# Summing the index scores over heads on TensorE with diagonal weight matrices, in a two-block transformer kernel

## The reference, cut to what matters

```python
dots = jnp.einsum('bthd,bsd->bths', qib.astype(f32), k_idx_f)
score = jnp.einsum('bths,bth->bts', jax.nn.relu(dots), wib.astype(f32)) * idx_scale
causal = key_pos[None, :] <= t[:, None]
score = jnp.where(causal[None], score, -jnp.inf)
_, sel = lax.top_k(score, top_k)
```

## Time and profile before

| what | value |
|---|---|
| median of 3 runs | 1260.83 us (1260.47 to 1261.44) |
| the profiled execution's own time | 1259.97 us |
| its span on the core | 1258.3 us |
| busy over the whole span | PE 82%, PEld 48%, DVE 35%, ACT 19%, POOL 3% |
| the stage of the change | about 495 us to 545 us from the span's start |

### The profile page before, as it was taken

How to read it: one execution, slowest core, us unless ns; L and a number is a source line. 1 busy time by engine, 2 the same in 40 slices (tenths; PEclk the granted TensorE clock), 3 DMA queues, 4 the chain that set the end, 5 groups by cost and what they waited for, 6 DMA issues and landing times.

```text
span 1258.3 us, 15368 instructions
## 1 busy us (share of the span) xinstructions
PE 1035.6 (82%) x6153; PEld 604.1 (48%) x6153; DVE 445.6 (35%) x1040; ACT 234.7 (19%) x576; POOL 41.7 (3%) x93
## 2 busy tenths in 40 slices
PE   5999999999999999978999999887474737464647
PEld 1788855444334448766888685632221303121213
DVE  0469827222221156976852462410010101010101
ACT  1233303111111232224512100310101101010101
POOL 0000000000000010100102300000000000000000
PEclk8899899999999999989999989897787878786878
DMA  9885957999999999323113236899999999999997
GB/s 364 283 329 204 395 182 308 394 429 427 427 431 428 416 344 393 125 77 125 68 43 139 102 105 268 344 383 423 425 421 426 419 429 421 429 420 429 419 428 290
DMA packets 80046, 406.13 MB, mean 323 GB/s; under 512 B 18713, under 2 KB 26198, under 8 KB 57336
## 3 DMA queue, kind: packets, MB, share of 16 engines
q1 hardware_dynamic: 79992, 405.38, 80.1%
HBM read 403.14 MB, written 2.23 MB: 322 GB/s over the span
## 4 chain that ended last, share of the span: by engine, by line
PE 58%; DMA 30%; DVE 8%; issue 1%; ACT 1%; SPq 1%; POOL 0%; DVEq 0%; ACTq 0%
DMA side<-in_expert_w_up 9%; PE ps L1742 8%; DMA side<-in_expert_w_down 7%; DMA side<-in_expert_w_gate 7%; PE ps L1331 5%; PE ps L714 5%; DMA ring<-in_expert_w_gate 4%; PE ps L1750 3%; PE ps L2800 3%; PE ps L2019 2%; PE ps L729 2%; PE ps L1731 2%; PE ps L3281 2%; DMA ring<-in_expert_w_up 2%; PE ps L1026 2%; PE ps L1385 2%
## 5 line engine op out<-in xcount | busy, mean ns | idle before, releaser
L1331 PE MATMUL ps<-ring,hT_sb 128*32 128x512 f32 x672 | 129.2, 740 | 161.2 <-DMA side<-in_expert_w_gate 53.4
L1331 PEld LDWEIGHTS ps<-ring,hT_sb 128*32 128x32 f32 x672 | 33.0, 133 | 251.8 <-issue 251.8
L1742 PE MATMUL ps<-ring,hT_sb 128*64 128x512 f32 x448 | 114.9, 599 | 2.9 <-DMA ring<-in_expert_w_gate 2.9
L1472 DVE TENSOR_TENSOR tmp<-ps,tmp 128x512 f32<-128x512 f32 x8 | 5.5, 692 | 187.5 <-ACT tmp L1460 187.5
L714 PE MATMUL ps<-hT_sb,ring 128*128 128x256 f32 x256 | 62.8, 397 | 2.7 <-DVE hT_sb L419 2.7
L1331 PE MATMUL ps<-side,hT_sb 128*32 128x512 f32 x224 | 65.0, 746 | 0.0
L1742 PEld LDWEIGHTS ps<-ring,hT_sb 128*64 128x64 f32 x448 | 35.7, 138 | 54.3 <-issue 54.2
L1451 ACT ACTIVATE hT_sb<-ps,modc 128x128 f32<-128x128 f32 x72 | 27.1, 457 | 178.1 <-PE ps L1312 178.1
L2019 PE MATMUL ps<-hT_sb,ring 128*128 128x256 f32 (+1 forms) x240 | 57.3, 392 | 0.0
L1750 PE MATMUL ps<-ring,tmp 128*64 128x512 f32 x256 | 56.7, 595 | 0.0
L714 PEld LDWEIGHTS ps<-hT_sb,ring 128*128 128x128 f32 x256 | 48.6, 197 | 14.0 <-issue 4.6
(11 more groups left out here) (539 smaller groups left out, 1615.9 us busy)
## 6 DMA issues: line engine op xcount, KB each, us to landing
ring<-in_expert_w_gate SPq DMA_DIRECT2D x12, 4096.0 KB, 20.3
ring<-in_expert_w_up SPq DMA_DIRECT2D x12, 4096.0 KB, 31.3
ring<-in_expert_w_down SPq DMA_DIRECT2D x22, 2048.0 KB, 17.4
ring<-in_expert_w_up SPq DMA_DIRECT2D x16, 2048.0 KB, 16.6
ring<-in_expert_w_down SPq DMA_DIRECT2D x7, 4096.0 KB, 20.2
ring<-in_expert_w_gate SPq DMA_DIRECT2D x12, 2048.0 KB, 19.0
side<-in_ada_w SPq DMA_DIRECT2D x20, 1024.0 KB, 7.0
ring<-in_w_in SPq DMA_DIRECT2D x9, 2048.0 KB, 10.3
```

The source lines that it names most:

```text
L1331: last = pe.matmul(bank[es, :], xg[:, c, es], w[e][:, c, :], start=(c == 0), stop=(c == KC - 1))
L1742: last = pe.matmul(bank[e * SLOTS:(e + 1) * SLOTS, :], xg[:, c, e * SLOTS:(e + 1) * SLOTS], dst(e, j, par)[:, c, :], start=(c == 0), stop= ...
```

## The change

The weighted sum over heads moves from DVE to PE. ACT makes, for each u, a 128x128 matrix with the head's weights of 128 tokens on its diagonal (the identity scaled per partition by `w_idx[:, u]`, into `more`); PE multiplies relu(u) by it and accumulates the eight heads of a token tile in one half of bank 3. So `dots` have banks 0 to 2 in place of 0 to 3, and dots u waits for relu u - 3. The four products of group m stand behind shifted product m. DVE copies both halves of bank 3 to `work` in one instruction at the head of the sparse stage (`take_scores`), which now also releases POOL's masks; PE waits for that copy before the key/value up-projection, which reuses bank 3.

```diff
         def dots(pe, u):
             t, h = u // 8, u % 8
             r = 32 * (h % 4)
-            if u >= 4:
-                pe.wait_ge(sem("idx_relu"), u - 3)
-            pe.matmul(ps[h % 4][:, 0:S], qiT[r:r + 32, h // 4, t * P:(t + 1) * P], kiT[r:r + 32, :],
+            if u >= 3:
+                pe.wait_ge(sem("idx_relu"), u - 2)
+            pe.matmul(ps[u % 3][:, 0:S], qiT[r:r + 32, h // 4, t * P:(t + 1) * P], kiT[r:r + 32, :],
                       start=True, stop=True).then_inc(sem("idx_dots"), 1)
 
+        def head_weight(u):
+
+            return more[:, 1024 + u * P:1024 + (u + 1) * P]
+
         def relu(act, u):
+            act.activation(head_weight(u), ident[:, :], ACT.Copy, scale=w_idx[:, u:u + 1])
             act.wait_ge(sem("idx_dots"), u + 1)
             if u >= RL:
                 act.wait_ge(sem("idx_added"), u - RL + 1)
-            act.activation(rl[:, u % RL, :], ps[u % 4][:, 0:S], ACT.Relu).then_inc(sem("idx_relu"), 1)
-
-        def add_head(v, u):
+            act.activation(rl[:, u % RL, :], ps[u % 3][:, 0:S], ACT.Relu).then_inc(sem("idx_relu"), 1)
+
+        def add_head(pe, u):
             t, h = u // 8, u % 8
-            v.wait_ge(sem("idx_relu"), u + 1)
-            w = w_idx[:, t * 8 + h:t * 8 + h + 1]
-            if h == 0:
-                ins = v.tensor_scalar(work[:, t, :], rl[:, u % RL, :], w, None, ALU.mult)
-            else:
-                ins = v.scalar_tensor_tensor(work[:, t, :], rl[:, u % RL, :], w, work[:, t, :], ALU.mult, ALU.add)
-            ins.then_inc(sem("idx_added"), 1)
-            v.wait_ge(sem("idx_added"), u + 1)
-            if h == 7:
-                v.tensor_copy(st6[:, 200 + t:201 + t], work[:, t, 0:1]).then_inc(sem("idx_score"), 1)
+            pe.wait_ge(sem("idx_relu"), u + 1)
+            pe.matmul(ps[3][:, t * S:(t + 1) * S], head_weight(u), rl[:, u % RL, :],
+                      start=(h == 0), stop=(h == 7)).then_inc(sem("idx_added"), 1)
+
+        def take_scores(v):
+
+            v.wait_ge(sem("idx_added"), 16)
+            v.tensor_copy(work, ps[3][:, :].rearrange("p (t s) -> p t s", t=NT)).then_inc(sem("idx_score"), 1)
...
                     shifted_product(pe, m)
+                    for u in range(4 * m, 4 * m + 4):
+                        add_head(pe, u)
                 for m in range(4, SHIFT_NOW):
...
                 act.wait_ge(sem("mixed_zero"), 1)
+                act.wait_ge(sem("pj_out"), at("pj_ki_out", 2))
                 for m in range(4):
...
                     sum_ada2_cols(v, k)
-                    for u in range(4 * (k - 4), 4 * (k - 4) + 4):
-                        add_head(v, u)
                     shifted_before(v, k - 4)
...
-                    pool.wait_ge(sem("idx_score"), t + 1)
+                    pool.wait_ge(sem("idx_score"), 1)
...
                 pe.wait_ge(sem("turn_out"), at("latT_done", 2))
 
+                pe.wait_ge(sem("idx_score"), 1)
                 for n in range(2):
...
+                take_scores(v)
                 turn_lat()
                 turn_q()
```

## The result

The changed kernel takes 1273.5 us (median of 4 runs, 1271.42 to 1276.37), the kernel before 1260.65 us beside it: ratio 1.0095, with a 95% interval of 1.0073 to 1.0117, or 9 to 15 us slower. The forecast was 1268.3 us, slower by 7.5 us, with a range up to 1271.8 us. The direction is right, the size too small.

The account below looks back on a forecast made before the run. PE and DVE were both taken as near their limit, PE 2.6 us ahead. Weight products 6.9 plus bank waits 3.4, less slack 2.6 and clock credit 0.2, gave +7.5: 1268.3 us, range 1264.0 to 1271.8.

Parts of the forecast that it names:

- the sum for the transposes of q: On PE up to q's transposes: weight products 6.9 us plus bank waits 3.4 us, so they come 10.3 us later.
- the wait for the third bank: On PE, every fourth dots waits for a relu: about 0.8 us in three groups, 1.0 in the first, 3.4 in all.
- the low clock in shifted product 0: On PE in shifted product 0: the 1.2 GHz stretch seen before, costing 1.8 us there; nothing added in the sum.
- DVE waits for them in `turn_lat`: On DVE between the scores' copy and `turn_lat`: idle for some 6 us, released by PE.
- PE's idle time before the transposes of k: On PE, waiting for DVE's norm of k: about 4 us in place of 6.74.
- The slack of 2.6 us: At q's transposes PE is 2.6 us ahead of DVE's need; that much delay is absorbed.
- The small credit of 0.2 us: Behind PE's idle stretch before k's transposes: a shorter stretch might keep the clock, worth 1.8 us; 0.2 counted.
- the weight products: On PE before q's transposes: 16 products at 0.435 us each, 6.9 us, with nothing to hide them.
- Rival A: PE has room, 4.7 of 25 us, so products cost 2.2 us: +3.0, 1263.8 us; 14%.
- rival B: DVE's relief decides and the kernel gets faster, to 1254.8 us at best, needing under 0.16 us a product; 3%.
- C: PE's clock falls at its stops: one more low stretch gives 1270.1 us; the large case, 1277 to 1285, has 6%.
- The ceiling of rival B: On DVE: 6.6 us of adds removed, 0.7 of copy added; 6 us gained if PE's transposes come soon enough.

Follow-up runs that it names:

- e1: The changed kernel with four banks for the dots again, the weight products kept: 1265.53 us, ratio 1.0029 against the kernel before.
- e2: The kernel before with three banks for the dots in place of four, DVE still adding the heads: 1264.42 us, ratio 1.0024.
- e3: The kernel before with DVE weighting one head, the seven other adds per token tile left out: 1258.12 us, ratio 0.9956.
- e4: The changed kernel with every fourth dots moved behind the shifted product of its group: 1270.22 us, ratio 1.0054 against the kernel before.
- e5: The changed kernel with the transposes of the latent and q ahead of shifted products 4 and 5: 1266.34 us, ratio 1.0039 against the kernel before.
- e6: The changed kernel with four banks for the dots and the transposes ahead of shifted products 4 and 5: 1260.47 us, ratio 0.9986 against before.
- e7: The kernel before with the transposes ahead of shifted products 4 and 5: 1262.4 us, ratio 0.9994.
- e9: The kernel of e6 with heads u = 0 to 3 added on DVE, the other twelve on PE: 1259.04 us, ratio 0.9984 against before.
- e8: The kernel of e6 with the 8-column head-weight products moved ahead of the index keys' full products: 1261.44 us, ratio 1.0000 against before.
- e10: The kernel of e9 with the 8-column products dealt out between the index keys' full products: 1256.95 us, ratio 0.9966 against before.
- e11: The kernel before with the 8-column products dealt out between the index keys' full products: 1264.6 us, ratio 1.0026.

## Why the prediction was right and wrong

*What failed.* The time lies above the range, 1273.5 us (1272.62 the second time) against 1271.8 at most. Two sizes in the sum for the transposes of q were wrong: the wait for the third bank, 3.4 us forecast and 4.6 measured, and the low clock in shifted product 0, which the sum had at nothing and which cost 1.5. So PE hands over 13.0 us later in place of 10.3, and the selection starts 10.35 later in place of 7.7. These two terms alone lift 1268.3 to 1271.0 us; the rest stays open, as said below.

*Right: the mechanism.* PE is full, its products delay the transposes, DVE waits for them in `turn_lat` (6.58 us, "some 6 us" forecast), and all but 2.6 us of the delay lands at the start of the selection. PE's idle time before the transposes of k is 4.10 us (about 4 forecast). The slack of 2.6 us holds in each kernel in which DVE waits: the changed one (13.0 becomes 10.35), e1 (6.97 becomes 4.32), e2 (6.85 becomes 4.2), and with the sign turned e3. In each of them, and in e4, the selection starts 1.61 us after the end of q's transposes; before it was 4.26. The small credit of 0.2 us for the clock behind the idle time was also about right: from the transposes of k to the attention scores it is 9.61 us, 9.66 before.

*Right: the weight products,* 6.9 us forecast, 4 x 1.73 measured. Rival A, room on PE because its weight loads are busy for 81% only, is refuted: each group of four products adds its full 1.72 us to the pace in e1. The rule of the Trainium skill's page "Perfetto Trace Analysis" (Identifying the Most-Contended Engine), by which that share, beside the share of the peak rate reached, tells the headroom, doesn't hold for this stretch of float32 products; the measurement decides.

*Wrong: the term for the wait for the third bank.* I gave the stop itself 0.6 to 1 us, measured 0.46 (0.43 in the first group), and wrote that "the shifted product about 0.17 later" would follow the fourth dots. It follows 0.63 us later. The 0.17 was a quarter of 0.71 us for four dots, but those run side by side, in four row ranges of the array, and the duration of the four is that of one. Splitting off the fourth pays that duration a second time: 1.15 us a group instead of 0.8, 4.6 us in all instead of 3.4. e4, where nobody waits, shows it by itself. The Trainium skill's page "TensorE: Matmul & The Clock Gate" (Part 3: Packing small matmuls — row/col tiling) says that products in different row groups overlap. The trace agrees: 0.62 alone, 0.64 for three, 0.65 for four. I had the row and divided it. The same division gave rival B its "cheapest product" of 0.18 us; a dots alone costs 0.62, more than the 0.43 of a product with 128 rows in a stream.

*Wrong: the clock in shifted product 0.* I put "one more low stretch" among the rivals (C) and not in the sum. It came: 6.31 us instead of 4.78, 1.5 us more. The sum at the transposes of q is 6.9 + 4.6 + 1.5 = 13.0, as measured. Whether the stops cause it is not shown: in the four traces with a stop in the first group the low stretch lasted 6.8 us (the changed kernel twice, e5) or 10 us (e2); in the seven others with the dots behind the small products it lasted 3.4 us six times (before, e1, e4, e6, e7, e9) and 6.8 us once (e3, whose PE runs the order of before). That speaks for the stops, with few traces; and in e2 and e5 the stretch had begun before the first stop. The stops in the later three groups did not bring the clock down: PEclk is 1.00 there in each of these traces. What causes it at all is shown better: the run of 8-column products, since it moved with them (e8) and was gone when they were dealt out (e10, e11), while PE's wait of 0.64 us ahead of the dots stayed.

*Open: the rest.* 10.35 us in the trace at the selection; in the total 12.9 and 11.2 by the medians, 12.0 and 10.7 by the ratios. The two profiled executions differ by 11.4: 0.6 ahead of the first dots, 10.35 up to the selection, 0.4 in all behind it. But the changed kernel's profiled execution was the fastest of its four, 2.1 below their median, and of the other three there is no trace. The trace of the repetition is 14.3 us longer than before, 10.4 of it up to the selection and some 4 behind. Between the transposes of k and the recurrence (the first issue of its block transfers) the changed kernel needed 1.6 us more than before in one trace and 6.1 more in the other, with a low-clock stretch near 600 us that the trace of before does not have. Such stretches stand at different places in the traces of other kernels too (near 587 us in e3 and e11), and what brings them is not known.

*The ceiling of rival B.* I wrote that DVE, relieved, "gains toward its 6 us" if PE's transposes come soon enough. In e3, where PE does nothing for it, the transposes stop DVE after 2.6 us. So the change had 2.6 us to win at this place, and cost PE 13.0.

## What to carry to other kernels

Before moving work to another engine, find that engine's next appointment with the one relieved: the slack between them (here 2.6 us) caps the gain, and every us of delay beyond it is paid in full. The products with 32 rows here run side by side and have together the duration of one, so don't price one of them by division, and look whether a buffer splits the group. And look at the order: the sixteen weight products with three banks cost 11 to 13 us, with four banks 3.7 (e1), and with the transposes moved ahead as well nothing (e6). Twelve of them were part of a kernel 4.5 us faster than before (e10): four banks, the transposes moved ahead, the first group left on DVE, the small products dealt out. Two of these edits alone, on the kernel before, did not gain (e7, e11). The two together on the kernel before were not run, so how much of the 4.5 us needs the weight products on PE is not shown.

## What the runs showed of the hardware

Behind a run of small products the granted clock fell, though PE was busy all through the run. Thirty-two MATMUL records of 8 columns took 3.63 us, with PE 100% busy. In all twelve traces in which they stand together, 1.2 GHz came during the last of them or within 2 us, for 3.4 us (six traces), 6.8 (five) or some 10 (e2). Dealt out between products of 256 columns, the clock stayed at 2.4 GHz (e10, e11). What this costs is no constant: with one order of PE's work (before, e3) shifted product 0 took 4.78 or 5.99 us.

Products with 32 rows in different row ranges cost 0.62 us for one, 0.64 for three and 0.65 for four, and float32 products with 128 rows that follow each other cost 0.43 each, with their weight loads busy for 81% of the time and no room left.

The times of one kernel spread by up to 11 us (1259.19 to 1269.81 in the kernel before, 1258.99 to 1267.8 in e11). Low stretches like the one near 600 us may be a part of that, which is not shown. So a single execution says little here about a few us, and the timeline, read from a common event, says more than the total.
